# PEER gate stage: the subtraction of the low halves moves from GpSimd to VectorE

## The chip, the cores and the metric

The kernel runs on one core of one Trainium2 chip. The metric is the device time of one launch in microseconds (us); lower is better. A core has five engines with a program each: TensorE (PE, matmuls), VectorE (DVE), ScalarE (ACT), GpSimd (Pool) and SyncE (SP, which here issues loads). They run side by side and meet through semaphores. Transfers between memory and the on-chip buffers are issued from SP, ACT and Pool, and all go through the core's 16 DMA engines.

## The reference, cut to what matters

The model has two layers; each ends with PEER, a retrieval of 16 of 16,384 one-neuron experts for each token and each of 8 heads:

```python
q = (x @ w_q).reshape(T, PEER_HEADS, 2, PEER_DQ_HALF)
...
best, pos = lax.top_k(cand, PEER_TOPK)
eidx = jnp.take_along_axis(cidx, pos, axis=-1)
gate = jax.nn.softmax(best, axis=-1)
...
hb = jax.nn.gelu(jnp.einsum('tkd,td->tk', u[ib], xb), approximate=False)
return jnp.einsum('tk,tkd->td', gb * hb, v[ib])
```

T is 640 tokens of 1024 values. The kernel does the last two lines in two ways. For 256 tokens ("sparse") it gathers the 128 chosen rows of `u`, and later of `v`, and works with them on VectorE. For the other 384 tokens ("dense") it computes the hidden value of every expert, as 128 tiles of 128 experts, and multiplies by a gate table that is zero where an expert was not chosen.

## The kernel before

PEER runs twice, once per layer, in four stages, each a block that begins and ends with a barrier of all engines: scores, select, gates, experts. The change is in the third, `peer_gates`.

**What the gate stage computes.** It builds the dense gate table. The 384 dense tokens are cut into 24 units of 16 tokens (NU, TU). For each unit VectorE makes four one-hot tiles of 128x2048 (`oh2`, `oh1`, `ohh`, `ohl`, lines 1079 to 1084), drains and signals `oh`. TensorE multiplies them for 16 tokens into a PSUM tile in two groups of 16 matmuls (lines 1100, 1101), ScalarE copies each group out (line 1140), and after two units stores 2 MB of the table.

**What else runs in it.** Two pieces of other stages fill the engines. First, 36 of the dense expert tiles get their hidden values early (class `EarlyHidden`), one tile in an even unit and two in an odd one (`tiles_of`). For a tile m, SP loads 512 KB of `u` into `ust`, two buffers (line 746, waiting for `ul`); ScalarE writes its rounded bf16 half `u_hi` (line 752, waiting for the load and for TensorE to be through with tile m-2); the low half `u_lo = ust - u_hi` is a subtraction of 128x1024 (line 756) that signals `ul`; TensorE runs 24 matmuls on the halves (line 792); ScalarE applies the GELU and stores the result (lines 768, 770). Second, 64 of the sparse dot products (class `SparseRows`): Pool issues gathers of 128 rows of 4 KB, 512 KB each, into a ring of eight row buffers (line 991), and VectorE takes a dot product with each (line 1005), about three in every unit but the first two.

**What sets the order.** Every engine runs its program in the order written. VectorE: for each unit its dot products, then the four one-hot tiles. TensorE: for each unit its 32 gate matmuls, then its tiles. ScalarE: a hand-written sequence of evacuations, GELUs and high halves. Pool: for each unit first the low halves of the unit's tiles, each of which waits for `uh` (its high half), then the gathers that refill the rows freed by the unit's dot products. SP: the 36 loads, each waiting for the low half of the tile before the last, which frees its buffer.

After the stage the experts stage starts with loads of its own; there VectorE makes the low halves itself (line 1345), with Pool issuing gathers all the while.

## Time and profile before

| | us |
|---|---|
| median of 3 runs | 4738.79 (4733.55 to 4744.9) |
| the profiled execution: its time | 4742.51 |
| the profiled execution: its span, first to last instruction | 4740.7 |
| gate stage of layer 1, first one-hot tile to end of the last | 1340.87 to 1601.93 |
| gate stage of layer 2, the same | 3487.86 to 3745.87 |

All times below are those of the profiled execution, counted from the start of its span. An engine's row gives when an instruction started, how long it took, its line, and in brackets how long the engine had been idle and what ended that. The share of busy time over the whole span (TensorE 85%, VectorE 67%, Pool 38%) is an average over stages with different limits, so the gate stage is read by itself.

### The profile page before, as it was taken

What the parts mean: (1) busy time and instruction counts of PE and PEld (TensorE: products, weight loads), DVE (VectorE), ACT (ScalarE), POOL (GpSimd) and SP (SyncE); (2) the same over time, 40 slices, a digit from 0 to 9 for tenths busy, and PEclk for the clock granted to TensorE, in tenths of its full rate; (3) what the DMA queues carried; (4) which work ended last, traced back from release to release, by engine and by line L of the source; (5) the groups of instructions that cost most, each with busy time, mean ns of one, the idle gap of its engine ahead of it and who ended that gap; (6) DMA issues with size and microseconds to landing.
All of it is one profiled execution on the core that took longest, in us unless ns stands there. A gap on an engine that the chain in (4) does not pass through costs nothing. (4 is left out here: it accounts for less than half of the span.)

```text
span 4740.7 us, 53729 instructions
## 1 busy us (share of the span) xinstructions
PE 4022.3 (85%) x18234; PEld 2300.0 (49%) x18234; DVE 3167.6 (67%) x5799; ACT 947.4 (20%) x1311; POOL 1802.5 (38%) x1188
## 2 busy tenths in 40 slices
PE   6998984997877799998898967897878799979898
PEld 2666663553445444443344555464445444433333
DVE  1455556366979777786665667267969777776665
ACT  1101100112345311110000245112445411100000
POOL 0000000003467677665562000003567577766552
PEclk7999996998989899998999989999988899989999
DMA  7111100115578899999996100113468899999996
GB/s 268 34 39 38 37 28 24 49 45 204 214 259 326 323 401 398 397 395 386 386 394 235 36 10 0 56 57 96 147 233 330 305 398 401 401 390 392 387 392 259
DMA packets 394670, 1086.71 MB, mean 229 GB/s; under 512 B 33664, under 2 KB 178304, under 8 KB 387968
## 3 DMA queue, kind: packets, MB, share of 16 engines
q0 software_dynamic: 147456, 536.94, 29.1%
q1 hardware_dynamic: 220544, 465.76, 28.0%
q10 hardware_dynamic: 26496, 81.80, 4.5%
q8 instruction: 96, 1.57, 0.1%
q14 instruction: 78, 0.64, 0.0%
HBM read 998.65 MB, written 85.72 MB: 229 GB/s over the span
## 5 line engine op out<-in xcount | busy, mean ns | idle before, releaser
L1264 PE MATMUL ex_ps_p<-ex_vst_p,ex_gh_p 128*128 128x512 f32 x3072 | 1382.3, 608 | 118.4 <-DMA ex_vst_p<-in_v 118.4
L1264 PEld LDWEIGHTS ex_ps_p<-ex_vst_p,ex_gh_p 128*128 128x128 f32 x3072 | 595.8, 196 | 849.4 <-issue 741.3
L756 POOL TENSOR_TENSOR eh_ulo_sl_p<-eh_ust_sl_p,eh_uhi_sl_p 128x1024 bf16<-128x1024 f32 x88 | 233.8, 2661 | 2035.1 <-ACT eh_uhi_sl_p L752 2035.1
L991 POOL DMA_INDIRECT sp_rows_p<-in_u,sidx_p x512 | 724.8, 1416 | 319.0 <-DVE sp_rows_p L1005 165.8
L991 POOL DMA_INDIRECT sp_rows_p<-in_v,sidx_p x512 | 655.9, 1281 | 432.1 <-DVE ex_acc_p L1017 305.5
L1005 DVE SCALAR_TENSOR_TENSOR sp_rows_p<-sp_rows_p,xs_p 128x1024 f32<-128x1024 f32 x512 | 684.4, 1374 | 69.4 <-DMA sp_rows_p<-in_u,sidx_p 61.2
L1017 DVE SCALAR_TENSOR_TENSOR ex_acc_p<-sp_rows_p,sp_gsp_p,ex_acc_p 128x1024 f32<-128x1024 f32 x512 | 643.7, 1283 | 49.6 <-DMA sp_rows_p<-in_v,sidx_p 15.0
L343 PE MATMUL rec_psA<-rec_hT,rec_wst 128*128 128x128 f32 (+1 forms) x1024 | 310.7, 451 | 50.8 <-DMA rec_wst<-in_rec_w_in 41.8
L792 PE MATMUL eh_psH_sl_p<-h_hi_p,eh_uhi_sl_p 128*128 128x384 bf16 x704 | 237.6, 337 | 78.2 <-POOL eh_ulo_sl_p L756 78.1
L792 PE MATMUL ex_ps_p<-h_hi_p,ex_uhi_p 128*128 128x384 bf16 x768 | 255.6, 333 | 56.7 <-DVE ex_ulo_p L1345 56.6
L628 PE MATMUL ps_psA_p<-ps_hT_p,ps_wst_p 128*128 128x128 f32 (+1 forms) x1024 | 287.3, 440 | 16.3 <-ACTq L168 16.3
L1357 DVE TENSOR_TENSOR ex_gh_p<-ex_est_p,ex_gst_p 128x384 f32<-128x384 f32 x160 | 89.2, 557 | 283.5 <-DMA ex_est_p<-hidden 183.7
L792 PE MATMUL ex_ps_p<-h_lo_p,ex_uhi_p 128*128 128x384 bf16 x768 | 255.5, 333 | 0.0
L792 PE MATMUL ex_ps_p<-h_hi_p,ex_ulo_p 128*128 128x384 bf16 x768 | 255.1, 332 | 0.0
L792 PE MATMUL eh_psH_sl_p<-h_hi_p,eh_ulo_sl_p 128*128 128x384 bf16 x704 | 236.8, 336 | 0.0
L792 PE MATMUL eh_psH_sl_p<-h_lo_p,eh_uhi_sl_p 128*128 128x384 bf16 x704 | 236.5, 336 | 0.0
L1100 PE MATMUL gt_ps_p<-gt_ohh_p,gt_oh_p 128*128 128x128 bf16 x768 | 120.1, 251 | 129.1 <-DVEq L1085 118.7
L1345 DVE TENSOR_TENSOR ex_ulo_p<-ex_ust_p,ex_uhi_p 128x1024 bf16<-128x1024 f32 x96 | 117.7, 1226 | 156.9 <-ACT ex_uhi_p L1301 147.9
L756 POOL TENSOR_TENSOR eh_ulo_gt_p<-eh_ust_gt_p,eh_uhi_gt_p 128x1024 bf16<-128x1024 f32 x72 | 187.8, 2616 | 90.3 <-ACT eh_uhi_gt_p L752 89.7
L628 PEld LDWEIGHTS ps_psA_p<-ps_hT_p,ps_wst_p 128*128 128x128 f32 x1024 | 155.0, 194 | 128.4 <-issue 125.4
L343 PEld LDWEIGHTS rec_psA<-rec_hT,rec_wst 128*128 128x128 f32 x1024 | 152.1, 199 | 129.1 <-issue 119.8
L1140 ACT ACTIVATE gt_gs_p<-gt_ps_p 128x1024 f32<-128x1024 f32 x96 | 181.0, 1991 | 152.0 <-PE gt_ps_p L1101 151.9
(242 smaller groups left out, 5822.8 us busy)
## 6 DMA issues: line engine op xcount, KB each, us to landing
ex_vst_p<-in_v SPq DMA_DIRECT2D x256, 512.0 KB
gates<-gt_gs_p ACTq DMA_DIRECT2D x24, 2048.0 KB
ex_ust_p<-in_uT SPq DMA_DIRECT2D x96, 512.0 KB
ex_gst_p<-gates SPq DMA_DIRECT2D x64, 768.0 KB
eh_ust_sl_p<-in_uT SPq DMA_DIRECT2D x88, 512.0 KB
eh_ust_gt_p<-in_uT SPq DMA_DIRECT2D x72, 512.0 KB
ex_est_p<-hidden SPq DMA_DIRECT2D x40, 768.0 KB
ada_wst<-in_ada_w SPq DMA_DIRECT2D x12, 2048.0 KB
```

Of the source, the lines that this page charges most:

```text
L343: last = nc.tensor.matmul(out, lhs, rhs, start=(k == 0), stop=(k == KD - 1))
L628: last = nc.tensor.matmul(psA[s % 2][:, col], wst[s][:, k, :], hT[:, k, tok], start=(k == 0), stop=(k == KD - 1))
L756: self.nc.gpsimd.tensor_tensor(self.u_lo[s][:], self.ust[s][:], self.u_hi[s][:], ALU.subtract).then_inc(self.ul, 1)
L792: last = nc.tensor.matmul(ps[:], a[:, k, :], b[:, k, :], start=(m == 0), stop=(m == len(prods) - 1))
L991: pool.indirect_dma_start(out=self.rows[n % self.NR][:], out_offset=None, in_=src, in_offset=bass.IndirectOffsetOnAxis(ap=self.sidx[:, b, ...
L1005: nc.vector.scalar_tensor_tensor(row[:], row[:], 1.0, self.xs[:, b, :], op0=ALU.mult, op1=ALU.mult, accum_out=self.hsp[:, b, k:k + 1]).the ...
L1017: nc.vector.scalar_tensor_tensor(to[:], row[:], self.gsp[:, b, k:k + 1], to[:], op0=ALU.mult, op1=ALU.add).then_inc(self.row_used, 1)
L1100: nc.tensor.matmul(o, oh1[r][:, at, :, e], ohh[r][:, at, :, e], start=True, stop=False)
L1140: nc.scalar.activation(gs[b % 2][:, :, TE * q:TE * q + TE].rearrange("p j t -> p t j"), ps[(4 * b + q) % 3][:], ACT.Copy).then_inc(ev, 1)
L1264: last = nc.tensor.matmul(psO[b][:, BANK * x:BANK * x + BANK], gh[q][:, P * b:P * b + P], vst[q][:, BANK * x:BANK * x + BANK], start=start ...
L1345: nc.vector.tensor_tensor(u_lo[n % 2][:], ust[n % 2][:], u_hi[n % 2][:], ALU.subtract).then_inc(ul, 1)
L1357: nc.vector.tensor_tensor(gh[q][:].rearrange("p (b t) -> p b t", t=TB), src.rearrange("p (b t) -> p b t", t=TB), gst[g % 2][:, :, q, :], A ...
```

## The change

The subtraction of the gate stage's 36 early tiles is issued by VectorE instead of Pool. VectorE does it one unit late: behind the one-hot tiles of unit n it makes the low halves of the tiles of unit n-1, and behind the last unit those of the last two tiles too. Pool keeps only the 72 gathers, in the same order; each still waits for its row buffer. The start value of `ul`, which lets SP begin to load, is now set by VectorE behind its first three small instructions instead of by Pool at the start of the block. TensorE's, ScalarE's and SP's programs are unchanged, and so are the select stage (its low halves stay on Pool) and the experts stage.

```diff
+    def take_low_dve(self, dve, m, s):
+        dve.wait_ge(self.uh, m + 1)
+        self.nc.vector.tensor_tensor(self.u_lo[s][:], self.ust[s][:], self.u_hi[s][:],
+                                     ALU.subtract).then_inc(self.ul, 1)
+
...
+            dve.sem_inc(eh.ul, 2)
             for n in range(NU):
...
                 dve.drain().then_inc(oh, 1)
+                if n > 0:
+                    for m in tiles_of(n - 1):
+                        eh.take_low_dve(dve, m, m % 2)
+            for m in tiles_of(NU - 1):
+                eh.take_low_dve(dve, m, m % 2)
...
         @block.gpsimd
         def _(pool):
-            eh.start_pool(pool)
-            for m in range(2):
-                for d in range(2):
-                    sparse.gather(pool, 2 * m + d)
-                eh.take_low(pool, m, m)
-            for d in range(4, sparse.NR):
+            for d in range(sparse.NR + first_dots):
                 sparse.gather(pool, d)
-            for u in range(NU):
-                for m in tiles_of(u):
-                    if m >= 2:
-                        eh.take_low(pool, m, m % 2)
-                for d in dots_of(u):
-                    sparse.gather(pool, sparse.NR + d)
```

VectorE's program around the third and fourth unit of the stage (units 2 and 3), before. A row is line, operation, output and inputs, output shape, and how often in a row; `sp_rows` are gathered rows, `gt_oh`, `gt_ohh`, `gt_ohl` one-hot tiles:

```order
L1005 SCALAR_TENSOR_TENSOR sp_rows_p,sp_hsp_p<-sp_rows_p,xs_p 128x1024 x2
L1079 TENSOR_TENSOR gt_oh_p<-gt_pk_p,gt_keyrow_p 128x2048
L1081 TENSOR_TENSOR gt_oh_p<-gt_pk_p,gt_keyrow_p 128x2048
L1083 TENSOR_TENSOR gt_ohh_p<-gt_oh_p,gt_pk_p 128x2048
L1084 TENSOR_TENSOR gt_ohl_p<-gt_oh_p,gt_pk_p 128x2048
L1005 SCALAR_TENSOR_TENSOR sp_rows_p,sp_hsp_p<-sp_rows_p,xs_p 128x1024 x3
```

The same place in the changed kernel, whose lines stand 5 or 6 further down:

```order
L761 TENSOR_TENSOR eh_ulo_gt_p<-eh_ust_gt_p,eh_uhi_gt_p 128x1024
L1010 SCALAR_TENSOR_TENSOR sp_rows_p,sp_hsp_p<-sp_rows_p,xs_p 128x1024 x2
L1085 TENSOR_TENSOR gt_oh_p<-gt_pk_p,gt_keyrow_p 128x2048
L1087 TENSOR_TENSOR gt_oh_p<-gt_pk_p,gt_keyrow_p 128x2048
L1089 TENSOR_TENSOR gt_ohh_p<-gt_oh_p,gt_pk_p 128x2048
L1090 TENSOR_TENSOR gt_ohl_p<-gt_oh_p,gt_pk_p 128x2048
L761 TENSOR_TENSOR eh_ulo_gt_p<-eh_ust_gt_p,eh_uhi_gt_p 128x1024 x2
L1010 SCALAR_TENSOR_TENSOR sp_rows_p,sp_hsp_p<-sp_rows_p,xs_p 128x1024 x3
```

One and two low halves now stand in turn between a unit's one-hot tiles and the next unit's dot products. At the end of the stage three of them stand behind the last one-hot tiles:

```order
L1089 TENSOR_TENSOR gt_ohh_p<-gt_oh_p,gt_pk_p 128x2048
L1090 TENSOR_TENSOR gt_ohl_p<-gt_oh_p,gt_pk_p 128x2048
L761 TENSOR_TENSOR eh_ulo_gt_p<-eh_ust_gt_p,eh_uhi_gt_p 128x1024 x3
L1042 UNCONDITIONAL_BRANCH
L1341 UNCONDITIONAL_BRANCH
```

So 33 of the 36 lie ahead of the signal for the last unit. Pool's program at the start of the stage, before:

```order
L991 DMA sp_rows_p<-in_u,sidx_p 128x1024 x2
L756 TENSOR_TENSOR eh_ulo_gt_p<-eh_ust_gt_p,eh_uhi_gt_p 128x1024
L991 DMA sp_rows_p<-in_u,sidx_p 128x1024 x2
L756 TENSOR_TENSOR eh_ulo_gt_p<-eh_ust_gt_p,eh_uhi_gt_p 128x1024
L991 DMA sp_rows_p<-in_u,sidx_p 128x1024 x4
L756 TENSOR_TENSOR eh_ulo_gt_p<-eh_ust_gt_p,eh_uhi_gt_p 128x1024 x2
L991 DMA sp_rows_p<-in_u,sidx_p 128x1024 x2
```

and in the changed kernel, where this is its whole program in the stage and the next rows leave it:

```order
L996 DMA sp_rows_p<-in_u,sidx_p 128x1024 x72
L1042 UNCONDITIONAL_BRANCH
L1042 ISA
```

No gather stands behind a low half any more.

## Rows read from the trace of the kernel before

**Rows 1.** Stretches: us, busy us of PE, PEld, DVE, ACT, POOL, clock, DMA share, GB/s

```profile
1340.00:1602.00 262.00, 194.72 (x1552) 133.53 (x1552) 255.34 (x226) 137.83 (x116) 201.53 (x107) 0.89 0.87 325
3487.00:3746.00 259.00, 198.43 (x1552) 136.78 (x1552) 251.13 (x226) 137.67 (x115) 194.45 (x104) 0.87 0.88 327
1625.00:1885.00 260.00, 252.84 (x1017) 128.46 (x1016) 205.07 (x324) 43.44 (x59) 179.11 (x129) 1.00 1.03 394
```

**Rows 2.** Waits in layer 1's gate stage, VectorE's then TensorE's: us, times, longest

```profile
DVE sp_rows_p L1005 <- DMA sp_rows_p<-in_u,sidx_p: 1.6, 2, 1.1
DVE gt_ohh_p L1083 <- issue: 0.4, 1, 0.4
...
PE gt_ps_p L1100 <- DVEq L1085: 61.2, 15, 12.7
```

**Rows 3.** Timeline of one unit of VectorE, layer 1: start, us, engine, line

```profile
1448.45 1.22 DVE L1079 TENSOR_TENSOR gt_oh_p<-gt_pk_p,gt_keyrow_p 128x2048 bf16<-128x2048 bf16 x1
...
1453.35 1.22 DVE L1005 SCALAR_TENSOR_TENSOR sp_rows_p<-sp_rows_p,xs_p 128x1024 f32<-128x1024 f32 x1
...
1454.50 1.22 DVE L1005 SCALAR_TENSOR_TENSOR sp_rows_p<-sp_rows_p,xs_p 128x1024 f32<-128x1024 f32 x1
...
1455.65 3.15 DVE L1005 SCALAR_TENSOR_TENSOR sp_rows_p<-sp_rows_p,xs_p 128x1024 f32<-128x1024 f32 x1
...
1458.72 1.21 DVE L1079 TENSOR_TENSOR gt_oh_p<-gt_pk_p,gt_keyrow_p 128x2048 bf16<-128x2048 bf16 x1
```

**Rows 4.** Timeline of Pool beside it

```profile
1455.34 2.37 POOL L756 TENSOR_TENSOR eh_ulo_gt_p<-eh_ust_gt_p,eh_uhi_gt_p 128x1024 bf16<-128x1024 f32 x1 [6.00 <-ACT eh_uhi_gt_p L752]
```

**Rows 5.** VectorE's groups by line, layer 1's gate stage: count, busy us, mean ns, idle before

```profile
L1005 DVE SCALAR_TENSOR_TENSOR sp_rows_p<-sp_rows_p,xs_p 128x1024 f32<-128x1024 f32 x64 | 116.2, 1860 | 4.2 <-DMA sp_rows_p<-in_u,sidx_p 1.6
L1084 DVE TENSOR_TENSOR gt_ohl_p<-gt_oh_p,gt_pk_p 128x2048 bf16<-128x2048 bf16 x24 | 40.7, 1698 | 0.0
L1083 DVE TENSOR_TENSOR gt_ohh_p<-gt_oh_p,gt_pk_p 128x2048 bf16<-128x2048 bf16 x24 | 39.0, 1625 | 2.2 <-issue 0.4
L1081 DVE TENSOR_TENSOR gt_oh_p<-gt_pk_p,gt_keyrow_p 128x2048 bf16<-128x2048 bf16 x24 | 34.9, 1455 | 0.0
L1079 DVE TENSOR_TENSOR gt_oh_p<-gt_pk_p,gt_keyrow_p 128x2048 bf16<-128x2048 bf16 x24 | 29.2, 1217 | 0.2
```

**Rows 6.** Timelines of VectorE: first and last one-hot tile of each gate stage

```profile
1340.87 1.23 DVE L1079 TENSOR_TENSOR gt_oh_p<-gt_pk_p,gt_keyrow_p 128x2048 bf16<-128x2048 bf16 x1
...
1600.72 1.21 DVE L1084 TENSOR_TENSOR gt_ohl_p<-gt_oh_p,gt_pk_p 128x2048 bf16<-128x2048 bf16 x1
...
3487.86 1.22 DVE L1079 TENSOR_TENSOR gt_oh_p<-gt_pk_p,gt_keyrow_p 128x2048 bf16<-128x2048 bf16 x1
...
3744.65 1.22 DVE L1084 TENSOR_TENSOR gt_ohl_p<-gt_oh_p,gt_pk_p 128x2048 bf16<-128x2048 bf16 x1
```

**Rows 7.** VectorE's groups in the experts stage, 1625 to 1885

```profile
L1005 DVE SCALAR_TENSOR_TENSOR sp_rows_p<-sp_rows_p,xs_p 128x1024 f32<-128x1024 f32 x132 | 156.5, 1221 | 20.9 <-DMA sp_rows_p<-in_u,sidx_p 20.2
L1345 DVE TENSOR_TENSOR ex_ulo_p<-ex_ust_p,ex_uhi_p 128x1024 bf16<-128x1024 f32 x29 | 35.5, 1226 | 32.7 <-ACT ex_uhi_p L1301 29.7 <-issue 0.5
```

**Rows 8.** Timelines of ScalarE and SP: ends of the two gate stages

```profile
1609.46 0.33 ACTq L1158 DMA_DIRECT2D gates<-gt_gs_p  x1
...
1617.85 0.82 SPq L1225 DMA_DIRECT2D ex_ust_p<-in_uT  x2
...
3751.85 0.33 ACTq L1158 DMA_DIRECT2D gates<-gt_gs_p  x1
...
3766.66 0.81 SPq L1225 DMA_DIRECT2D ex_ust_p<-in_uT  x2
```

**Rows 9.** Timelines of SP and ScalarE: two loads of a tile, and its high half

```profile
1366.78 0.33 SPq L746 DMA_DIRECT2D eh_ust_gt_p<-in_uT  x1
...
1373.68 1.06 ACT L752 ACTIVATE eh_uhi_gt_p<-eh_ust_gt_p 128x1024 bf16<-128x1024 f32 x1 [1.61 <-DMA eh_ust_gt_p<-in_uT]
...
3508.22 0.33 SPq L746 DMA_DIRECT2D eh_ust_gt_p<-in_uT  x1
...
3518.76 1.06 ACT L752 ACTIVATE eh_uhi_gt_p<-eh_ust_gt_p 128x1024 bf16<-128x1024 f32 x1 [0.92 <-DMA eh_ust_gt_p<-in_uT]
```

**Rows 10.** Transfers in layer 1's gate stage (1340 to 1602): GB/s in 40 slices

```profile
GB/s 316 238 279 334 405 250 295 383 351 243 405 416 184 333 411 358 283 359 268 265 357 395 268 243 346 414 336 377 418 139 356 408 299 273 394 415 159 348 412 253
```

## The prediction, made before the changed kernel was run

> **What bounds the kernel now.** I read the gate stages by themselves, since only they change: first the busy time by stretch. In both, VectorE is busy nearly all the time: 255.34 of 262 us in layer 1, 251.13 of 259 in layer 2 [rows 1]. No other engine comes near: TensorE 194.72, ScalarE 137.83, and Pool's 201.53 are not on VectorE's way as work. The list of waits says the same from both sides: once started, VectorE waits 1.6 us for gathered rows and 0.4 us for anything else, while TensorE waits 61.2 us, 15 times, for VectorE's one-hot tiles [rows 2]. So the stage ends when VectorE has worked through its list, and what the list costs is what the stage costs.
>
> Next I ask what VectorE's time is made of, from its timeline. The four one-hot tiles of a unit take 4.90 us (1448.45 to the start of the first dot product, 1453.35), and an undisturbed dot product 1.15 us (1453.35 to 1454.50) [rows 3]. The third one takes 3.15 us instead of 1.22, and the next instruction starts 3.07 us after it: 1.92 us too late. In that time Pool runs a subtraction of a low half, 1455.34 to 1457.71 [rows 4]: VectorE's instruction started 0.31 us behind it and could not proceed. The groups by line show that this is the rule. Free of stalls, 64 dot products at 1.22 us are 78.1 us; they took 116.2. Three of the four one-hot lines took 40.7, 39.0 and 34.9 us where the fourth took 29.2 [rows 5]. The excess is 38.1 + 11.5 + 9.8 + 5.7 = 65.1 us, for 36 subtractions of Pool.
>
> **The change, part by part.** *Stalls removed.* VectorE's list without stalls, up to the end of the last one-hot tile, is 24 x 4.90 + 64 x 1.15 = 117.6 + 73.6 = 191.2 us. It took 261.1 us in layer 1 (1340.87 to 1601.93) and 258.0 in layer 2 (3487.86 to 3745.87) [rows 6]. Of the difference, 69.9 and 66.8 us, 2.0 us are the waits of layer 1 [rows 2]; for layer 2 I allow 3. That leaves 67.9 and 63.8 us of stalls, 1.9 and 1.8 us for each of 36 subtractions, near the 1.92 of the one looked at and a little over the 65.1 of the groups.
>
> *Work added to VectorE.* The experts stage has the same subtraction on VectorE, of the same shape and types: 1226 ns each [rows 7], the length of a one-hot tile or a dot product to within 10 ns, so I take the same step of 1.15 us from start to start. The bounds are 1.14 and, if each pays the gap that the first dot product behind a drain pays ((4.2 - 1.6)/24 = 0.1 by the idle time in [rows 5]), 1.23 + 0.1 = 1.33; I take 1.15 since a subtraction stands where the dot product stood. 33 of the 36 lie ahead of the last one-hot signal: 33 x 1.15 = 38.0 us (37.6 to 43.9). The stage's list becomes 191.2 + 2 + 38.0 = 231.2 us in layer 1 and 191.2 + 3 + 38.0 = 232.2 in layer 2. That is 29.9 and 25.8 us less.
>
> *What else has to fit under 231 us.* TensorE's 194.72 us [rows 1] are all but the last unit's matmuls and the last two tiles, so some 210 us in all; shared out by columns (24 matmuls of 384 for a tile, 32 of 128 for a unit; 34 tiles and 23 units in the stretch) a tile takes 4.4 us and a unit's gate matmuls 2.0, an estimate. ScalarE's 138 us grow little, and Pool drops to its gathers. All have room.
>
> *The tail.* Now TensorE has tile 33 still in front of it when the last one-hot tiles are ready, since its low half comes behind them: 1.2 us for the low half and 4.4 for the product before the last 32 gate matmuls can run. ScalarE makes the last high half in the meantime, then copies out the last two groups and issues the last 2 MB store. That store left 7.5 us (1609.46 - 1601.93) and 6.0 us (3751.85 - 3745.87) behind VectorE's end, and the experts stage's first loads followed 8.4 and 14.8 us after it [rows 8]. With 5.6 us put ahead of the matmuls I put the tail, from VectorE's last one-hot tile on, at 4 us longer in layer 1, where it was longer by itself, and 5 in layer 2 (0 to 6 each). Nothing covers it: it is paid.
>
> *New waits on VectorE.* Each subtraction waits for ScalarE's high half, and behind it queue the dot products and the next unit's one-hot tiles, for which TensorE waits. With two `ust` buffers, the load for tile m+2 can start only when VectorE has made the low half of tile m. The tight links are those where the next use comes one unit later, 1.15 + 3 x 1.15 + 4.90 = 9.5 us; there are two in every two units, 24 in a stage. Needed are 0.2 us to the issue, the load, 1.06 us for the high half and about 0.2 to start: a load of up to 8.0 us costs nothing. One load took 6.9 us (1366.78 to 1373.68), the longest that I found 10.5 (3508.22 to 3518.76) [rows 9], which would hold VectorE for 2.5 us. I take 3 us in a stage, about one link in twenty at the longest; the bounds are 0 and 10 (one in six). Moving the first load of the stage behind VectorE's first small instructions delays it by about 2 us, but the first low half is wanted only 10 us into the stage: nothing.
>
> *Transfers.* The same 85 MB (325 GB/s x 262 us, [rows 1]) now have to move in 231 us: 368 GB/s instead of 325. In the busiest of the 40 slices of the stage 405 to 418 GB/s passed [rows 10], and the experts stage holds 394 GB/s for 260 us [rows 1]; so there is room, some 10%, and I charge nothing beyond the 3 us. There is one rule that speaks against this: the Trainium skill, "DMA: Bandwidth & Descriptors", section "Where 436 GB/s comes from", says that between memory and the on-chip buffers the memory side binds, at about 358 GB/s for a core. By it the stage could not fall below 85 MB / 358 GB/s = 238 us, some 6.5 us more in each layer: 4711 us instead of the sum below. The 394 GB/s of this trace do not bear it out, so the sum stays as it is.
>
> *Sum.* Layer 1: -29.9 + 4 + 3 = -22.9. Layer 2: -25.8 + 5 + 3 = -17.8. Together -40.7, and the stages that follow start behind a barrier, so they simply begin earlier. The profiled execution took 4742.5 us, 3.7 more than the median of 4738.8. On the scale of the median: 4738.8 - 40.7 = **4698 us**.
>
> **The rivals.** *Transfers become the bound.* Prefetching is shallow here (two tile buffers, eight rows), and the slices of the stage vary between 139 and 418 GB/s. If the average rises only to 345 GB/s, half way, the stretch takes 247 us, 15 less than now; after the longer tail 11 remain in each layer: about 4717 us. It decides from any average below 368. (The skill's rule above would be a case of this one.) Against it: the 394 of the experts stage. It would show as VectorE waiting for gathered rows, as it does there for 20.2 us beside 132 dot products [rows 7].
>
> *The buffer loop becomes the bound.* If ordinary loads get slower because the queues are fuller, each of the 24 tight links costs load minus 8.0 us. At 9.0 us the gain of about 23 us a stage is used up: no change, 4739. At the longest load seen in every link, 10.5, it is 60 us a stage against 23: 4739 + 2 x 37 = 4813, clearly slower. For it: the chain is in the program and VectorE has no slack to hide it. Against it: the common load is at 7 us, and a longer unit lowers the demand on the transfers again, so a loss well past the gain is unlikely.
>
> *The stalls stay.* If they came from Pool's issuing of gathers and not from its subtractions, VectorE would get 38 us more and lose nothing, 42 us a stage with the tail: 4823. Against it: 132 dot products of the experts stage have a mean of 1221 ns while Pool issues 129 gathers in the same stretch [rows 1, 7].
>
> **How the numbers follow.** The forecast gets 0.66, transfers as the bound 0.17, the loop 0.15 (0.08 near no change, 0.07 slower), stalls that stay 0.02. Faster by over 0.2% (9.5 us, about what a measurement of this kernel can tell from no change) is then 0.83, no change 0.08, slower 0.09. Low end of the range: 55.7 us from the two lists, the 5 us of remaining waits gone too, no tail and no new wait: 4678. High end: the second case and its misses, 4723.
>
> **What would show it.** In the gate stages of the changed kernel, no dot product or one-hot tile of about 3 us on VectorE; 72 subtractions on it at 1.23 us; Pool with gathers alone. From the first one-hot tile to the last, 231 to 238 us, with VectorE's remaining idle time under 10 us a stage and put down to the high halves; 350 to 370 GB/s. The experts stages keep their length. I would be wrong if VectorE's idle time in a stage were over 20 us: put down to gathered rows, the first rival; to ScalarE's high half, the second. Dot products of 3 us beside gathers would be the third.

## The result, and the profile after

The changed kernel takes 4702.4 us (median of six executions, 4699.2 to 4710.2) where the kernel before takes 4739.8 (six, 4733.6 to 4744.9): a ratio of 0.9925, with a 95% interval of 0.9912 to 0.9938, or 37.4 us less. The forecast was 4698 us, 41 less. A repeat gave 4698.2 us beside 4743.9 for the kernel before: 0.9902 (0.9886 to 0.9919), or 45.7 us less. Both intervals lie wholly below 0.998, the 0.2% from which the prediction calls a kernel faster, and the forecast gain lies between the two measured ones.

The stretches of the two gate stages, from VectorE's small first instructions to its last one-hot tile, and of layer 1's experts stage: us, busy us of PE, PEld, DVE, ACT, POOL, clock, DMA share, GB/s. They answer to [rows 1].

```profile
1342.00:1578.00 236.00, 191.12 (x1503) 126.44 (x1504) 227.03 (x261) 131.02 (x111) 107.16 (x72) 0.90 0.96 356
...
3465.00:3703.00 238.00, 191.83 (x1528) 126.59 (x1528) 227.48 (x261) 131.90 (x112) 107.28 (x72) 0.90 0.95 353
...
1627.00:1887.00 260.00, 253.49 (x997) 127.52 (x995) 204.81 (x325) 41.18 (x56) 175.95 (x136) 0.99 1.03 399
```

The stretch has shrunk by some 24 us and VectorE still fills it: 227 of 236 us. Pool's time fell from 201.53 us to 107.16, which are its 72 gathers. The transfers went up from 325 to 356 GB/s.

VectorE's groups by line in layer 1's stretch (1342 to 1578): count, busy us, mean ns, idle time before. They answer to [rows 5].

```profile
L1010 DVE SCALAR_TENSOR_TENSOR sp_rows_p<-sp_rows_p,xs_p 128x1024 f32<-128x1024 f32 x64 | 74.9, 1220 | 0.0
L761 DVE TENSOR_TENSOR eh_ulo_gt_p<-eh_ust_gt_p,eh_uhi_gt_p 128x1024 bf16<-128x1024 f32 x34 | 41.0, 1224 | 6.7 <-ACT eh_uhi_gt_p L752 4.0
L1089 DVE TENSOR_TENSOR gt_ohh_p<-gt_oh_p,gt_pk_p 128x2048 bf16<-128x2048 bf16 x24 | 29.4, 1225 | 1.9
L1085 DVE TENSOR_TENSOR gt_oh_p<-gt_pk_p,gt_keyrow_p 128x2048 bf16<-128x2048 bf16 x24 | 29.3, 1221 | 0.2
L1090 DVE TENSOR_TENSOR gt_ohl_p<-gt_oh_p,gt_pk_p 128x2048 bf16<-128x2048 bf16 x24 | 29.3, 1220 | 0.0
L1087 DVE TENSOR_TENSOR gt_oh_p<-gt_pk_p,gt_keyrow_p 128x2048 bf16<-128x2048 bf16 x24 | 29.3, 1220 | 0.0
```

Every group is at its undisturbed length now: the dot products at 1220 ns instead of 1860, the last one-hot line at 1220 instead of 1698. The new subtractions take 1224 ns, as those of the experts stage did [rows 7]. The only wait left is one on ScalarE's high halves, 4.0 us in all.

TensorE's waits in layer 1's gate stage, which answer to the last line of [rows 2]:

```profile
PE eh_psH_gt_p L797 <- DVE eh_ulo_gt_p L761: 34.2, 14, 3.6
PE gt_ps_p L1111 <- DVEq L1091: 10.9, 1, 10.9
```

TensorE still waits for VectorE and for hardly anything else: at the start of the stage once for a one-hot tile, and from then on for low halves.

The first and the last one-hot tile of each stage, from VectorE's timeline (start, us, engine, line), as in [rows 6]:

```profile
1344.12 1.23 DVE L1085 TENSOR_TENSOR gt_oh_p<-gt_pk_p,gt_keyrow_p 128x2048 bf16<-128x2048 bf16 x1
...
1576.12 1.22 DVE L1090 TENSOR_TENSOR gt_ohl_p<-gt_oh_p,gt_pk_p 128x2048 bf16<-128x2048 bf16 x1
...
3467.09 1.23 DVE L1085 TENSOR_TENSOR gt_oh_p<-gt_pk_p,gt_keyrow_p 128x2048 bf16<-128x2048 bf16 x1
...
3700.56 1.22 DVE L1090 TENSOR_TENSOR gt_ohl_p<-gt_oh_p,gt_pk_p 128x2048 bf16<-128x2048 bf16 x1
```

From the first start to the last end the list takes 233.2 us in layer 1 and 234.7 in layer 2; before it was 261.1 and 258.0.

What gave some of this back stands behind the list: the end of layer 1's stage, first VectorE's timeline, with its idle time and what ended it in brackets,

```profile
1577.46 1.23 DVE L761 TENSOR_TENSOR eh_ulo_gt_p<-eh_ust_gt_p,eh_uhi_gt_p 128x1024 bf16<-128x1024 f32 x1
1584.28 1.23 DVE L761 TENSOR_TENSOR eh_ulo_gt_p<-eh_ust_gt_p,eh_uhi_gt_p 128x1024 bf16<-128x1024 f32 x1 [5.59 <-ACT eh_uhi_gt_p L752]
1587.32 1.23 DVE L761 TENSOR_TENSOR eh_ulo_gt_p<-eh_ust_gt_p,eh_uhi_gt_p 128x1024 bf16<-128x1024 f32 x1 [1.82 <-ACT eh_uhi_gt_p L752]
```

then ScalarE's and SP's (the load of tile 35 first, layer 2's first load of the experts stage last), which answer to [rows 8].

```profile
1578.87 0.33 SPq L746 DMA_DIRECT2D eh_ust_gt_p<-in_uT  x1
...
1579.70 3.70 ACT L1140 ACTIVATE gt_gs_p<-gt_ps_p 128x1024 f32<-128x1024 f32 x2 [1.40 <-PE gt_ps_p L1112]
1583.19 1.06 ACT L752 ACTIVATE eh_uhi_gt_p<-eh_ust_gt_p 128x1024 bf16<-128x1024 f32 x1
...
1586.23 1.06 ACT L752 ACTIVATE eh_uhi_gt_p<-eh_ust_gt_p 128x1024 bf16<-128x1024 f32 x1 [1.61 <-DMA eh_ust_gt_p<-in_uT]
1587.19 3.69 ACT L1140 ACTIVATE gt_gs_p<-gt_ps_p 128x1024 f32<-128x1024 f32 x2
1590.95 0.33 ACTq L1158 DMA_DIRECT2D gates<-gt_gs_p  x1
...
1599.36 0.81 SPq L1225 DMA_DIRECT2D ex_ust_p<-in_uT  x2
...
3723.38 0.81 SPq L1225 DMA_DIRECT2D ex_ust_p<-in_uT  x2
```

The last 2 MB store follows the last one-hot tile by 13.6 us (1590.95 - 1577.34), where it was 7.5; the first load of the experts stage follows by 22.0 us, where it was 15.9. In layer 2 these are 13.2 (6.0 before) and 21.6 (20.8 before).

### The profile page after: what moved, and what is told of

Read it like the earlier page. It is cut to its first block and busy times, and to the rows that moved or that the text cites. A ratio compares the mean times of both kernels' runs of the same rounds, so it can differ in the third digit from the quotient of the medians.

```text
span 4703.1 us, 53727 instructions
## 1 busy us (share of the span) xinstructions
PE 4027.0 (86%) x18234; PEld 2294.1 (49%) x18234; DVE 3121.8 (66%) x5871; ACT 945.7 (20%) x1311; POOL 1592.2 (34%) x1116
## 5 line engine op out<-in xcount | busy, mean ns | idle before, releaser
L996 POOL DMA_INDIRECT sp_rows_p<-in_u,sidx_p x512 | 711.0, 1389 | 566.4 <-DVE sp_rows_p L1010 420.5
L1022 DVE SCALAR_TENSOR_TENSOR ex_acc_p<-sp_rows_p,sp_gsp_p,ex_acc_p 128x1024 f32<-128x1024 f32 x512 | 643.7, 1283 | 55.1 <-DMA sp_rows_p<-in_v,sidx_p 22.5
L1010 DVE SCALAR_TENSOR_TENSOR sp_rows_p<-sp_rows_p,xs_p 128x1024 f32<-128x1024 f32 x512 | 606.3, 1222 | 57.8 <-DMA sp_rows_p<-in_u,sidx_p 52.9
L628 PE MATMUL ps_psA_p<-ps_hT_p,ps_wst_p 128*128 128x128 f32 (+1 forms) x1024 | 285.9, 438 | 16.3 <-ACTq L168 16.3
L797 PE MATMUL eh_psH_gt_p<-h_hi_p,eh_uhi_gt_p 128*128 128x384 bf16 x576 | 202.0, 351 | 70.0 <-DVE eh_ulo_gt_p L761 68.1
L797 PE MATMUL eh_psH_gt_p<-h_hi_p,eh_ulo_gt_p 128*128 128x384 bf16 x576 | 201.6, 350 | 0.0
```

The source lines that it names most:

```text
L628: last = nc.tensor.matmul(psA[s % 2][:, col], wst[s][:, k, :], hT[:, k, tok], start=(k == 0), stop=(k == KD - 1))
L797: last = nc.tensor.matmul(ps[:], a[:, k, :], b[:, k, :], start=(m == 0), stop=(m == len(prods) - 1))
L996: pool.indirect_dma_start(out=self.rows[n % self.NR][:], out_offset=None, in_=src, in_offset=bass.IndirectOffsetOnAxis(ap=self.sidx[:, b, ...
L1010: nc.vector.scalar_tensor_tensor(row[:], row[:], 1.0, self.xs[:, b, :], op0=ALU.mult, op1=ALU.mult, accum_out=self.hsp[:, b, k:k + 1]).the ...
L1022: nc.vector.scalar_tensor_tensor(to[:], row[:], self.gsp[:, b, k:k + 1], to[:], op0=ALU.mult, op1=ALU.add).then_inc(self.row_used, 1)
```

## The experiments

All kernels are the changed one with the edit shown; line numbers shift by an edit's length. "List" is the time from the first one-hot tile's start to the last one's end, as above; "first load" is the issue of the experts stage's first load behind that end. Beside the single executions the kernel before took 4734.2 and 4740.4 us, once each.

| kernel | us (executions) | list, layers 1 / 2 | first load after it |
|---|---|---|---|
| before | 4739.8 (6) | 261.1 / 258.0 | 15.9 / 20.8 |
| before, again | 4747.8 (1) | 259.0 / 259.2 | 21.4 / 17.6 |
| after | 4702.4 (6) | 233.2 / 234.7 | 22.0 / 21.6 |
| after, again | 4698.2 (4) | 233.0 / 234.4 | 22.2 / 22.0 |
| Pool subtracts idly | 4840.2 (1) | 304.1 / 305.2 | 21.5 / 21.3 |
| Pool fills | 4695.2 (1) | 234.2 / 233.9 | 21.6 / 21.9 |
| Pool copies | 4752.9 (1) | 259.7 / 260.6 | 22.0 / 21.3 |
| no low halves | 4666.9 (1) | 217.0 / 217.7 | 22.9 / 22.2 |
| low halves first | 4710.3 (4) | 245.8 / 243.9 | 16.3 / 14.4 |
| low halves in the middle | 4701.5 (1) | 239.1 / 241.5 | 17.9 / 17.3 |
| three input buffers | 4693.3 (4) | 232.8 / 234.7 | 20.9 / 20.5 |
| three buffers, low first | 4707.7 (6) | 246.4 / 247.2 | 16.0 / 14.3 |
| high half early | 4705.0 (4) | 238.4 / 235.4 | 21.4 / 22.2 |
| three buffers, high half early | 4696.0 (6) | 234.5 / 234.3 | 20.1 / 20.3 |

### The kernel before, once more

> The kernel before, profiled a second time, to see how far stage lengths vary from one execution to the next. In the two profiles at hand the gate stages became 21.7 and 22.5 us shorter (from VectorE's first instruction in the stage to the first load of the experts stage: 279.3 to 257.6, 281.1 to 258.6), but the span only 37.6: 3.2 us came back ahead of the first gate stage and 5.6 us in layer 2's experts stage (974.1 to 979.7). My theory, that only the gate stages changed and the rest is scatter: the gate stages here again 279 and 281 within 3 us, and the start of the first one and layer 2's experts stage anywhere within 6 us of either value. Rival, that the change costs something in the stages around it: the first gate stage starts again at 1338.6 within 1 us and layer 2's experts stage takes again 974 us within 2.

4747.8 us. Its lists agree with the first profile's (261.1 and 258.0) to 2.1 us. Its way from the last one-hot tile to the first load does not: 21.4 and 17.6 us against 15.9 and 20.8. The tail of the kernel before scatters by 5 us, so it has to be averaged before it is compared. The first gate stage begins at 1346.3 us, later than in either profile, and layer 2's experts stage takes 973.6 us, as in the first; that it took 979.7 with the change is not the change's doing, since the changed kernel's repeat, below, shows 973.8.

### Pool subtracts again, into nothing

```
-            for d in range(sparse.NR + first_dots):
+            for d in range(sparse.NR):
                 sparse.gather(pool, d)
+            for u in range(NU):
+                for m in tiles_of(u):
+                    pool.wait_ge(idled, m)
+                    nc.gpsimd.tensor_tensor(idle[:], sparse.xs[:, 0, :], sparse.xs[:, 1, :],
+                                            ALU.subtract).then_inc(idled, 1)
+                for d in dots_of(u):
+                    sparse.gather(pool, sparse.NR + d)
```

> The changed kernel, with 36 subtractions of 128x1024 given back to Pool in each gate stage, between its gathers as before, for which nobody waits (inputs are token rows that rest in on-chip memory, the output a tile that nobody reads). VectorE keeps its 36 low halves. Theory (VectorE is held up by Pool's subtractions, 1.9 us each): VectorE's list from first to last one-hot tile goes from 233.2 us to about 233 + 36 x 1.8 = 298 us in each layer, instructions of about 3 us are back on it, and the program takes 4702 + 2 x 63 = 4828 us (4800 to 4840). Rival (the stalls came from Pool's issuing of gathers, or from Pool's program order): no change, 4702 within 10.

4840.2 us. VectorE's program and all waits on data are those of the changed kernel; only the 36 subtractions on Pool, whose result nobody reads, came in. Pool's timeline, then VectorE's, in one unit of layer 1:

```profile
1458.78 2.58 POOL L1126 TENSOR_TENSOR gt_idle_p<-xs_p 128x1024 bf16<-128x1024 f32 x1
```

```profile
1457.92 1.23 DVE L1090 TENSOR_TENSOR gt_ohh_p<-gt_oh_p,gt_pk_p 128x2048 bf16<-128x2048 bf16 x1
1459.06 3.38 DVE L1091 TENSOR_TENSOR gt_ohl_p<-gt_oh_p,gt_pk_p 128x2048 bf16<-128x2048 bf16 x1
```

The one-hot tile that starts 0.28 us behind Pool's subtraction takes 3.38 us, and it ends 1.08 us after Pool's end at 1461.36. It is the picture of [rows 3, 4], where the held instruction ended 1.09 us after Pool's (1458.80 - 1457.71). In each layer 36 VectorE instructions were lengthened, by 75 and 76 us together, 2.1 us each. That gives back the stalls and keeps the added work: what was forecast for "the stalls stay" (4823 us), and a little worse since this subtraction takes 2.8 us in the mean where the old one took 2.6.

### Pool fills, and Pool copies

The same places, but in one kernel a fill, which reads nothing, and in the other a copy, which reads one tile:

```
-                    nc.gpsimd.tensor_tensor(idle[:], sparse.xs[:, 0, :], sparse.xs[:, 1, :], ALU.subtract).then_inc(idled, 1)
+                    nc.gpsimd.memset(idle[:], 0.0).then_inc(idled, 1)
```

```
+                    nc.gpsimd.tensor_copy(idle[:], sparse.xs[:, 0, :]).then_inc(idled, 1)
```

> The same as the run before it, but each of the 36 extra Pool instructions only fills the idle tile with zeros (128x1024 bf16): it writes on-chip memory and reads none. If any Pool instruction on data holds VectorE up for as long as it runs, stalls of about the length of the fill come back, 36 in a stage, and the program gets slower by 72 times that length. If it is the reading that collides, no instruction of VectorE is longer than 1.3 us and the program stays at 4702 within 10. The Trainium skill, 'SBUF - State Buffer', section 'Who interferes with whom', says the second: a VectorE instruction with two inputs in on-chip memory collides with a GpSimd instruction that reads it, not with one that only writes. I expect the second.

> The changed kernel with 36 extra Pool instructions a gate stage for which nobody waits, like the two runs with subtractions and fills: here each copies 1024 values per partition of a token row (float32) into the idle tile (bf16), so it has one input in on-chip memory. If it is Pool's reading that holds VectorE up, stalls are back, each about as long as the copy runs beside it (36 in a stage; at 1 to 2 us each 4770 to 4840 us in all). If only Pool instructions with two inputs do it, no instruction of VectorE is longer than 1.3 us and the program stays at 4700 within 10. After the fill, which did not hold VectorE up at all, I expect the first.

The fill left the time where it was, 4695.2 us; the copy brought it to 4752.9. Pool's and VectorE's groups in layer 1, first with the fill,

```profile
L1126 POOL MEMSET gt_idle_p<- 128x1024 bf16 x36 | 34.6, 962 | 0.8
```

```profile
L1091 DVE TENSOR_TENSOR gt_ohl_p<-gt_oh_p,gt_pk_p 128x2048 bf16<-128x2048 bf16 x24 | 29.3, 1220 | 0.0
```

then with the copy.

```profile
L1126 POOL CAST gt_idle_p<-xs_p 128x1024 bf16<-128x1024 f32 x36 | 55.2, 1532 | 1.0
```

```profile
L1010 DVE SCALAR_TENSOR_TENSOR sp_rows_p<-sp_rows_p,xs_p 128x1024 f32<-128x1024 f32 x64 | 76.5, 1243 | 0.0
L761 DVE TENSOR_TENSOR eh_ulo_gt_p<-eh_ust_gt_p,eh_uhi_gt_p 128x1024 bf16<-128x1024 f32 x36 | 50.2, 1415 | 13.9 <-ACT eh_uhi_gt_p L752 11.4
L1091 DVE TENSOR_TENSOR gt_ohl_p<-gt_oh_p,gt_pk_p 128x2048 bf16<-128x2048 bf16 x24 | 47.7, 1989 | 0.0
```

Beside 36 fills no VectorE instruction of the list is longer than 1.3 us; beside 36 copies 35 are, by 27 us in a layer, 0.77 us each, and the list grows by 26.5 us (259.7 - 233.2). The copies' time lies under the 4770 us that were expected at least, since a stall is shorter than the copy. So it is neither Pool being busy nor its writing that holds VectorE, but its reading. VectorE's instructions here all have two inputs; one with a single input was not tried. The Trainium skill, "SBUF — State Buffer", section "Who interferes with whom", says this: a VectorE instruction with two inputs in on-chip memory contends with a GpSimd instruction that reads that memory, and not with one that only writes it. These runs agree, with the three prices 2.1, 0.77 and 0 us.

### The low halves left out

```
-        self.nc.vector.tensor_tensor(self.u_lo[s][:], self.ust[s][:], self.u_hi[s][:],
-                                     ALU.subtract).then_inc(self.ul, 1)
+        dve.sem_inc(self.ul, 1)
...
+            for s in range(2):
+                nc.vector.memset(eh.u_lo[s][:], 0.0)
+            dve.drain()
```

> The changed kernel without the 72 subtractions: VectorE waits for the high half and signals the low half without making it (the low halves stay zero, so a part of each early tile's product is left out; TensorE does the same matmuls). Theory (VectorE's list still sets the stage): it loses 33 x 1.15 = 38 us ahead of the last one-hot tile, 233 to 195, until the next limit catches it, TensorE's 210 us of work or 85 MB of transfers at the experts stage's 394 GB/s, 216 us: the stage becomes 13 to 25 us shorter in each layer and the program takes 4655 to 4680. Rivals (transfers or the two-buffer loop set it already): VectorE's time goes into waits and the program stays within 10 of 4702.

4666.9 us. The list fell to 217.0 and 217.7 us, not to 195: 16 and 17 us less for 38 us of work taken out. What is late then, from the waits of VectorE and ScalarE in layer 1's stretch 1340 to 1555 (us, times, longest) and its busy times:

```profile
DVE sp_rows_p L1009 <- ACT eh_uhi_gt_p L752: 25.9, 11, 5.3
```

```profile
ACT eh_ge_gt_p L772 <- DMA hidden<-eh_ge_gt_p: 27.9, 10, 5.2
ACT eh_uhi_gt_p L752 <- DMA eh_ust_gt_p<-in_uT: 22.9, 13, 14.0
```

```profile
1340.00:1555.00 215.00, 181.39 (x1488) 122.59 (x1489) 184.60 (x224) 130.59 (x110) 104.44 (x70) 0.93 0.99 382
```

VectorE waits for high halves, and ScalarE for transfers, whose engines are busy 0.99 of the time at 382 GB/s. So by these rows the bound under VectorE's list is transfers, and it lies at about 217 us; no run loosened it to test that. The rival "transfers become the bound" was then 16 us away from deciding in the changed kernel.

### The changed kernel again, and other places for the low halves

> The changed kernel once more, as the yardstick on the same chip for the three runs beside it, and for a second profile of its tail. Expected: about 4702 us (4695 to 4710); both gate stages 258 us from VectorE's first instruction to the first load of the experts stage, the last 2 MB store 13 us behind the last one-hot tile.

4698.2 us, with lists of 233.0 and 234.4 and first loads 22.2 and 22.0 us behind them: stage and tail repeat to 0.4 us.

In one kernel the low halves of unit n - 1 stand at the head of unit n, in another between its dot products and its one-hot tiles:

```
             for n in range(NU):
                 r = n % RING
+                if n > 0:                       # first
+                    for m in tiles_of(n - 1):
+                        eh.take_low_dve(dve, m, m % 2)
                 for d in dots_of(n):
                     sparse.step(dve, d)
+                if n > 0:                       # middle (in place of the one above)
+                    for m in tiles_of(n - 1):
+                        eh.take_low_dve(dve, m, m % 2)
...
                 dve.drain().then_inc(oh, 1)
-                if n > 0:
-                    for m in tiles_of(n - 1):
-                        eh.take_low_dve(dve, m, m % 2)
```

> The changed kernel with the low halves of unit n-1 at the head of unit n, ahead of its dot products, instead of behind its one-hot tiles. 34 instead of 33 low halves then lie ahead of the last one-hot tiles, so VectorE's list is 1.2 us longer; but tile 33 is multiplied while VectorE makes the last one-hot tiles, and the last 32 gate matmuls no longer wait behind it. If the 13 us from the last one-hot tile to the last store are TensorE's tile 33 in front of those matmuls, as the prediction had it, the store comes at 6 to 8 us as before the change, and the program gains 2 x 3 to 2 x 5 us: 4692 to 4697. Rival, that the tail is ScalarE's order (the last high half in front of the last two copies) or the transfers: the store stays at 12 to 14 us and the program at 4702 within 4.

> The changed kernel with the low halves of unit n-1 between the dot products and the one-hot tiles of unit n: 3.4 us later than at the head of the unit (there VectorE's list took 245.8 and 243.9 us), 4.9 us earlier than behind the one-hot tiles (233.2 and 234.7). If the 10 us that the head cost are waits for ScalarE's high halves, which come too late for an earlier place, this one lies between, 236 to 242 us with 4 to 9 us of such waits, and the last store again 6 to 8 us behind the last one-hot tile; the stage as a whole within 3 us of 258. Rival: the head was slow for another reason (what stands ahead of the dot products), then the list is 235.

At the head: 4710.3 us, ratio 0.9937 (0.9919 to 0.9955), no better than the changed kernel. Half of the expectation held: with tile 33 out of the way of the last gate matmuls the last store follows the list by 7.5 and 6.0 us, as in the kernel before. (The load of tile 35 is out of the way too in this kernel, so the run doesn't tell the two apart; the timelines do, below.) But the list grew to 245.8 and 243.9. VectorE's waits in layer 1's list:

```profile
DVE eh_ulo_gt_p L761 <- ACT eh_uhi_gt_p L752: 14.5, 8, 4.7
```

In the middle the list is 239.1 and 241.5 us, as expected, and the store comes 9.5 and 8.9 us after it, where 6 to 8 were expected: 4701.5 us. The earlier the low halves stand, the shorter the tail and the longer the list; what decides is how long VectorE lets ScalarE's high halves lie before it asks for them.

### Three input buffers

If those waits came from the two-buffer loop (load, high half, low half), a third `ust` buffer would remove them. The edit is a ring of three for the input tiles of the gate stage, on all engines:

```
-        self.ust = [sb(f"eh_ust{s}", [P, KD, P]) for s in range(2)]
+        self.ust = [sb(f"eh_ust{s}", [P, KD, P]) for s in range(nu)]
...
-        pe.wait_ge(self.ul, m + 3)
+        pe.wait_ge(self.ul, m + 1 + self.nu)
...
-            eh.loop_sp(sp, tiles)
+            for m in range(tiles):
+                eh.sp(sp, m, m % 3)
```

> The changed kernel with three input buffers for the early tiles of the gate stage instead of two, so that a load can start one tile earlier. If the waits of VectorE for high halves (4.0 and 5.3 us ahead of the last one-hot tile, 7.4 and 7.0 behind it, in the profile of the changed kernel) come from the two-buffer loop, the waits in the list go (4 to 5 us less a stage), some of those behind it too: 4688 to 4695 us. If they come from the load on the transfers or from ScalarE's order, no change: 4702 within 4.

> Both together: low halves at the head of the next unit, and three input buffers. If the two act in different places (tail, list) the gains add: 4680 to 4690 us, a ratio to the kernel before of about 0.989. If they remove the same wait, no better than the better of the two.

4693.3 us, 0.9892 (0.9877 to 0.9908), with the low halves where the change put them, and 4707.7 us, 0.9918 (0.9902 to 0.9933), with them at the head. The first is the fastest of the kernels that leave nothing out, but its interval overlaps that of the changed kernel's repeat, 0.9886 to 0.9919; the stages are 1.6 and 1.2 us shorter than the repeat's. Its time lies in the range expected, 4688 to 4695, but not for the reason given: the waits in the list did not go. The buffer did what it was to do on ScalarE, whose waits in layer 1's list are, in the changed kernel and then with three buffers,

```profile
ACT eh_uhi_gt_p L752 <- DMA eh_ust_gt_p<-in_uT: 32.0, 12, 9.5
```

```profile
ACT eh_uhi_gt_p L762 <- DMA eh_ust_gt_p<-in_uT: 9.6, 1, 9.6
```

and VectorE waits as before, 4.0 us without it and this with it:

```profile
DVE eh_ulo_gt_p L766 <- ACT eh_uhi_gt_p L762: 3.8, 3, 2.6
```

With the low halves at the head it still waits 16.1 us with three buffers (in the slowest of that kernel's executions, 4729.5 us, the one profiled), against 14.5 with two, and the gains don't add up. So the expectation of these two failed on one point: within the list, loads are not what VectorE waits for. What the third buffer gains stands behind the list, where the last store comes 12.5 and 12.1 us after it instead of 13.6 and 13.2.

### High halves earlier on ScalarE

ScalarE's and VectorE's timelines at the longest wait of the changed kernel's list suggested another cause:

```profile
1480.33 3.76 ACT L1140 ACTIVATE gt_gs_p<-gt_ps_p 128x1024 f32<-128x1024 f32 x2 [6.84 <-PE gt_ps_p L1112]
1483.89 1.05 ACT L752 ACTIVATE eh_uhi_gt_p<-eh_ust_gt_p 128x1024 bf16<-128x1024 f32 x1
```

```profile
1481.35 1.22 DVE L1090 TENSOR_TENSOR gt_ohl_p<-gt_oh_p,gt_pk_p 128x2048 bf16<-128x2048 bf16 x1
1484.98 1.23 DVE L761 TENSOR_TENSOR eh_ulo_gt_p<-eh_ust_gt_p,eh_uhi_gt_p 128x1024 bf16<-128x1024 f32 x1 [2.41 <-ACT eh_uhi_gt_p L752]
```

The high half starts as soon as ScalarE is through with two evacuations of gate products, 3.76 us, that stand ahead of it in its program. If that order is the cause, the wait goes when the high half is put ahead of them, with two buffers or with three:

```
+                if b > 0:
+                    high(m + 1)
                 rows(b, 0)
                 rows(b, 1)
-                if b > 0:
-                    high(m + 1)
                 gelu(m)
```

> The changed kernel with one line of ScalarE's program moved: the first high half of each group of three tiles stands ahead of the two evacuations of gate products that it stood behind. Theory (VectorE's remaining waits come from ScalarE's order): the list loses most of its 4.0 and 5.8 us of waits, 229.5 to 231.5 us where it was 233; the wait of 5.6 us for the last but one high half behind the list is gone, and the last store comes some 3 us sooner; 4 to 6 us a stage, 8 to 12 in all: about 4688 to 4694. Rival (the loads are just late): ScalarE now waits for the load ahead of the evacuations, these come later, TensorE waits for them, and the list stays at 233 us or grows: 4700 to 4712.

> The same line moved in the kernel with three input buffers, where ScalarE's waits for loads are nearly gone (9.6 us, once). Theory (ScalarE's order): list 229.5 to 231 us, tail as in the kernel with two buffers or a little shorter; 4684 to 4691. If loads are what is late in the kernel with two buffers, this one alone gains. If neither moves the list from 233 us, the cause of the remaining waits is neither loads nor this place in ScalarE's order.

It doesn't. 4705.0 us, 0.9910 (0.9887 to 0.9934), and with three buffers 4696.0, 0.9896 (0.9877 to 0.9916); no list is shorter than the changed kernel's by more than 0.4 us, and the store comes 13.0 and 13.8 us after it with two buffers, no sooner. The theory of ScalarE's order falls for the list. With two buffers time and list came out as its rival, late loads, would have them, but with three, where loads come early, the list is no shorter either; so neither explains the waits. VectorE's one long wait of layer 1's list with two buffers, and TensorE's first gate matmul ahead of it:

```profile
1495.98 1.23 DVE L761 TENSOR_TENSOR eh_ulo_gt_p<-eh_ust_gt_p,eh_uhi_gt_p 128x1024 bf16<-128x1024 f32 x1 [7.49 <-ACT eh_uhi_gt_p L752]
```

```profile
1485.45 0.29 PE L1111 MATMUL gt_ps_p<-gt_ohh_p,gt_oh_p 128*128 128x128 bf16 x1 [6.47 <-issue]
```

The same pause of TensorE stands ahead of the wait in the changed kernel, once in each stage,

```profile
1476.71 0.23 PE L1111 MATMUL gt_ps_p<-gt_ohh_p,gt_oh_p 128*128 128x128 bf16 x1 [3.75 <-issue]
...
3601.79 0.23 PE L1111 MATMUL gt_ps_p<-gt_ohh_p,gt_oh_p 128*128 128x128 bf16 x1 [3.47 <-issue]
```

and also in the kernel before.

```profile
1479.89 0.29 PE L1100 MATMUL gt_ps_p<-gt_ohh_p,gt_oh_p 128*128 128x128 bf16 x1 [5.02 <-issue]
...
3626.92 0.28 PE L1100 MATMUL gt_ps_p<-gt_ohh_p,gt_oh_p 128*128 128x128 bf16 x1 [5.17 <-issue]
```

"issue" says that TensorE waited for nothing that the profile shows; this unit's one-hot tiles had been ready since 1463.59 in the changed kernel's layer 1. Behind pauses of 3.47 to 5.01 us stand VectorE's waits of 3.1 to 4.7 us (3.75 and 3.47 with 3.1 and 4.4 in the changed kernel, 4.27 with 4.7 here in layer 2, 5.01 and 3.75 with 4.7 and 4.0 with three buffers besides), not in order of length, and behind the one of 6.47 one of 7.5. The way from the one to the other is in the program: evacuations and the next high half on ScalarE wait for TensorE, and the low half for the high half. It is argued from there and was not tested.

The place of the pause is the same in all 28 gate stages of the 14 profiles: ahead of matmul 817 of the stage. There TensorE's program jumps back: it is a loop of two rounds of 12 units (`pe.Fori(0, NBL // SPAN)`, line 1102 of the changed kernel), and this matmul is the first of the second round. In all 28, too, a 16 KB transfer of the kind "instruction" ends 1.5 to 1.8 us before that matmul starts (1475.01 and 1476.71 in the changed kernel's layer 1), whether the pause took 1.4 us or 6.5. So the traces point to TensorE's program being fetched for the second round. The other transfers of this kind in a stage, 14 of 15 in the changed kernel's layer 1, mostly pass without such a pause; and no run was made with the loop unrolled, so the cause is not shown.

## Why the prediction was right, and where its terms were off

**The mechanism** held in each part. VectorE's list sets the stage: taking the added work out makes the list 16 and 17 us shorter, and the stage 14 and 15, before anything else is late, and lengthening its instructions by 75 us (Pool subtracts idly) lengthens the stage by 70 (327.9 - 257.6 from VectorE's first instruction of the stage to the first load). The stalls came from Pool's subtractions, not from its gathers: they are gone with 72 gathers still issued, back with idle subtractions, and absent beside fills.

**The list.** Forecast were 231.2 and 232.2 us with 3 us of new waits on top, 234.2 and 235.2 in all; measured 233.2 and 234.7. Less its waits (4.0 us, and 5.8 in layer 2) layer 1's list is 229.2 us, and the working of the prediction without its allowances gives 24 x 4.90 + 64 x 1.15 + 33 x 1.15 = 229.2. All stalls of [rows 5, 6] went, and a subtraction costs the step of 1.15 us.

**The new waits.** Their size was nearly right (4.0 and 5.3 us for 3), their cause was not. The prediction derived them from slow loads in the loop through two buffers. The third buffer took ScalarE's waits for loads from 32.0 us to 9.6 and left VectorE's at 3.8. The step that failed is the one that counted the tight links by load time alone: most of the wait, 3.1 of 4.0 us in layer 1 and 4.4 of 5.3 in layer 2, follows TensorE's one pause at the second round of its loop. The rival built on that loop (4739 to 4813 us) rested on a cause that is hardly at work here: the third buffer moved the lists by 0.4 and 0.0 us.

**The tail.** Its first part was right, in cause and size: tile 33 in front of the last gate matmuls. The end of the last one in layer 1, before and after the change:

```profile
1605.38 0.31 PE L1101 MATMUL gt_ps_p<-gt_ohl_p,gt_oh_p 128*128 128x128 bf16 x1
```

```profile
1585.12 0.22 PE L1112 MATMUL gt_ps_p<-gt_ohl_p,gt_oh_p 128*128 128x128 bf16 x1
```

That is 3.8 us behind the list before and 8.0 after; in layer 2 it is 2.2 and 7.3. So the matmuls end 4.2 and 5.1 us later, against 4 and 5 put down. In layer 1 that is a little luck: they start 5.8 us later, behind the gate matmuls of the unit before as well, but run 2.0 us instead of 3.6. But the store came 6.1 and 7.2 us later than before, over the bound of 6. The step that failed is that ScalarE makes the last high half in the meantime. It can't: the load of tile 35 is issued only when low half 33 has freed its buffer (1578.87), ScalarE waits for it 1.61 us (0.93 in layer 2), and the last two evacuations stand behind that high half. They begin 1.8 and 2.1 us after the last matmul, where they followed it at once before. With three buffers and the high half early they begin 0.2 us after it, and the store comes 11.7 and 11.9 us behind the list. So here, and not in the list, the loop through two buffers costs something. The way to the first load grew less: over both executions of each kernel from 18.9 us (15.9, 20.8, 21.4, 17.6) to 22.0 (22.0, 21.6, 22.2, 22.0), by 3.1 us, since before it ended in a wait that scatters. Against the single profile of before it is +6.1 and +0.8.

**The transfers.** 356 and 353 GB/s passed in the stretch, inside the 350 to 370 forecast, and VectorE never waited for a row. That rate alone cannot tell the free run from the rule of the Trainium skill that the prediction weighed ("DMA: Bandwidth & Descriptors", section "Where 436 GB/s comes from", about 358 GB/s for a core). The same stage without the low halves can: 382 GB/s over 215 us, and the experts stage 399 over 260. The rule does not bind here, and the measurement decides.

**The sum.** The stages, from VectorE's first instruction to the first load, became 21.7 and 22.5 us shorter, 44.2 together, against 22.9 and 17.8, 40.7 together, forecast. Between the two profiled spans (4740.7 and 4703.1) lie 37.6 us; the other 6.5 arose outside the gate stages (+3.2 ahead of the first, -2.3 between them, +5.6 in layer 2's experts stage). The edit does not touch these stretches, and in the other runs they scatter as much: the first gate stage begins between 1337.5 and 1355.3 us, and layer 2's experts stage takes 973.6 to 981.2. So the 4 us between forecast and median are within what one execution differs from another, and that the sum came so near is in part luck: the stages gained 3.5 us more than forecast, and scatter elsewhere took more than that back. One reading of the prediction was off without weight: TensorE's whole work comes to 205.5 us by its own rates (194.72 + 2.0 + 2 x 4.4), not 210.

## What to carry to other kernels

Work that is put on Pool to spare a busy VectorE can cost VectorE more than it would have done itself: look on VectorE's timeline for instructions of a known length that are long exactly beside Pool's, and count them (here 1.9 us of stall for each 1.15 us of work spared). When the long ones are gone, make the new list out of undisturbed steps from start to start; it came out to 0.1 us. A wait that a moved instruction brings is not explained by the engine that it names: take away each thing that this engine waits for in turn (here loads, then its order) before one of them is called the cause. Where a pause keeps its place in the program while its time shifts, read what the program does at that place.

## What the runs showed of the hardware that was not expected

- A held VectorE instruction seems not to have begun: it ends 1.07 to 1.09 us after Pool's ends, in all 280 lengthened instructions of the lists of four kernels (before, its repeat, idle subtractions, copies), whether Pool's took 2.37 us (before) or 2.58 (idle subtraction). So each stall is about Pool's duration less the time by which VectorE started later (0.3 us in many, up to 1.3) and less 0.14 (1.22 - 1.08), which for the old kernel's [rows 3, 4] gives 2.37 - 0.31 - 0.14 = 1.92 us, as measured there.
- A copy on Pool with a single input is enough to hold VectorE (0.77 us for a copy of 1.53 us); a fill of the same tile, 0.96 us, is not.
- TensorE makes one pause in each gate stage, of 3.5 to 6.5 us (1.4 and 1.7 where Pool subtracts idly), at the jump of its program's loop, and goes on 1.5 to 1.8 us after a 16 KB transfer of the kind "instruction" has ended. This holds in all 28 gate stages; in 27 the trace names no releaser, in one (layer 2 of the kernel before, repeated) VectorE. In the changed kernel most of what VectorE still waits for in the list follows this pause.
